# A decoder layer on one core: two side tiles moved from the delta solve to the convolution, and the first of them split by VectorE

## What is computed

```
proj = xn @ w_in                                   # one combined input projection
qkv, gate_a, b, a, q_b, k_b, v_b, gate_b, sel_a, sel_b = split(proj)
qkv = silu(causal_conv(qkv, conv_w, width 4))      # 12 channel tiles of 128
q, k = l2norm(q), l2norm(k)
o_a = gated_delta(q, k, v, beta, logd)             # chunks; (L + I)^-1 per chunk and head
...                                                # retention on q_b, k_b, v_b; merge; experts
```

## Time and profile before

| | |
|---|---|
| median of 3 runs | 2220.53 us (2217.37 to 2221.3) |
| the profiled execution | 2223.61 us, its span 2221.8 us |
| TensorE busy | 1816.8 us (82%) |
| VectorE busy | 1311.0 us (59%) |
| ScalarE busy | 878.0 us (40%) |
| GpSimd busy | 635.9 us (29%) |
| convolution | from 159.6 to 258.05 us |
| delta solve | from 258.05 to 438.3 us |

### The profile page before, as it was taken

The page is one execution under the profiler, slowest core; times in us unless marked ns, Lnnn a source line. Parts: engine busy times, 40 slices in busy tenths (PEclk is TensorE's granted clock), DMA queues, the critical chain, the costliest instruction groups (busy, mean ns, idle before and its releaser), DMA issues.

```text
span 2221.8 us, 25857 instructions
## 1 busy us (share of the span) xinstructions
PE 1816.8 (82%) x8652; PEld 1172.6 (53%) x8652; DVE 1311.0 (59%) x2832; ACT 878.0 (40%) x2277; POOL 635.9 (29%) x553
## 2 busy tenths in 40 slices
PE   5988889979987897899887777777777777777776
PEld 4988889969967887565542222222223222222222
DVE  2228363353364527677866766767667866766764
ACT  4223312242244224444444444444444444444443
POOL 0003012100000002454434344444444443444442
PEclk8999899979997997999999999999999999999999
DMA  3413112236015229999999999999999999999997
GB/s 102 126 42 92 34 51 72 76 106 201 26 67 191 94 75 369 332 405 410 419 393 420 417 419 420 420 419 416 404 420 400 419 419 419 406 420 420 420 410 294
DMA packets 171790, 636.84 MB, mean 287 GB/s; under 512 B 12531, under 2 KB 97590, under 8 KB 104713
## 3 DMA queue, kind: packets, MB, share of 16 engines
q0 software_dynamic: 74880, 545.29, 60.0%
q1 hardware_dynamic: 96784, 89.98, 13.0%
HBM read 617.39 MB, written 17.93 MB: 286 GB/s over the span
## 4 chain that ended last, share of the span: by engine, by line
DMA 31%; PE 12%; ACT 8%; DVE 8%; issue 3%; POOL 0%; DVEq 0%; POOLq 0%; ACTq 0%
DMA ex_uv_row<-in_peer_uv,ex_eidx 31%; PE ps L2037 9%; DVE ex_uv_row L2270 5%; ACT ex_spread L2129 2%; ACT L2119 2%; ACT L2113 1%; ACT ret_tables L2124 1%; PE ps L612 1%; PE ps L614 1%; PE ps L613 1%; ACT ret_tables L2119 1%; DMA ex_uv_row<-in_peer_uv,ex_eidx_s 1%; DVE ex_sel L2242 0%; DVE ex_sel L2246 0%; DVE ex_best L2245 0%
## 5 line engine op out<-in xcount | busy, mean ns | idle before, releaser
L2037 PE MATMUL ps<-ex_uv_row,ex_spread 128*128 128x512 f32 (+1 forms) x2020 | 964.7, 611 | 278.9 <-ACT ex_spread L2129 276.6
L1996 POOL DMA_INDIRECT ex_uv_row<-in_peer_uv,ex_eidx x512 | 564.3, 1102 | 999.7 <-PE ps L2037 711.4
L2270 DVE CUSTOM_DVE_ANT_0 ex_uv_row<-ex_uv_row,x_ffn 128x1024 f32<-128x1024 f32 x512 | 623.9, 1224 | 361.4 <-DMA ex_uv_row<-in_peer_uv,ex_eidx 355.6
L2037 PEld LDWEIGHTS ps<-ex_uv_row,ex_spread 128*128 128x128 f32 (+1 forms) x2020 | 351.5, 189 | 852.7 <-issue 852.4
L2119 ACT ACTIVATE ret_tables<-ret_tables 128x1 f32<-128x1 f32 x520 | 104.9, 202 | 645.7 <-DVE ret_tables L2270 644.2
L2129 ACT ACTIVATE ex_spread<-square,ret_tables 128x128 f32<-128x128 f32 (+1 forms) x505 | 201.9, 400 | 16.6
L2124 ACT ACTIVATE ret_tables<-ret_tables 128x1 f32<-128x1 f32 x512 | 150.6, 294 | 17.0
L612 PE MATMUL ps<-proj_b_whi,x_lo 128*128 128x256 f32 (+1 forms) x320 | 91.0, 285 | 7.6 <-DVE proj_b_wlo L521 7.0
L612 PE MATMUL ps<-x_hi,ex_w_lo 128*128 128x260 f32 (+1 forms) x272 | 90.7, 333 | 6.3 <-DVE x_lo L2313 3.3
L614 PE MATMUL ps<-proj_b_whi,x_hi 128*128 128x256 f32 (+1 forms) x320 | 90.6, 283 | 0.0
L613 PE MATMUL ps<-proj_b_wlo,x_hi 128*128 128x256 f32 (+1 forms) x320 | 90.5, 283 | 0.0
(11 more groups left out here) (409 smaller groups left out, 3245.3 us busy)
## 6 DMA issues: line engine op xcount, KB each, us to landing
first_raw<-in_w_in SPq DMA_DIRECT2D x8, 1024.0 KB, 8.3
ex_uv_row<-in_peer_uv,ex_eidx POOLq DMA_INDIRECT x512
dp_w_raw<-in_w_in SPq DMA_DIRECT2D x14, 512.0 KB, 4.3
proj_a_raw<-in_w_in SPq DMA_DIRECT2D x4, 1024.0 KB, 5.2
cv_w_raw<-in_w_in SPq DMA_DIRECT2D x8, 512.0 KB
proj_b_raw<-in_w_in SPq DMA_DIRECT2D x4, 1024.0 KB, 5.7
S_sample<-in_state_ret SPq DMA_DIRECT2D x1, 4096.0 KB, 22.4
out_ret_s<-S_sample SPq DMA_DIRECT2D x4, 1024.0 KB, 4.4
```

Of the source, the lines that this page charges most:

```text
L1996: pool.indirect_dma_start(uv_row[:, p % RING, :], None, a["peer_uv"][0], bass.IndirectOffsetOnAxis(ap=index_of(n), axis=0)).then_inc(row_l ...
L2037: ins = pe.matmul(k.pv[j % 2][0:r, c, :], spread[:, p % RING, 0:r], uv_row[:, p % RING, D + c * 512:D + (c + 1) * 512], start=first, stop= ...
L2270: dve.tensor_tensor_reduce(u, u, x, 1.0, 0.0, ALU.mult, ALU.add, coef[:, n:n + 1]).then_inc(dotted, 1)
```

## The change

Two side tiles go from `delta_solve` to `convolve`: 10 there and 12 in the solve. In `convolve` the first tile's split is done by VectorE, as the first instruction of its program, where GpSimd did it; GpSimd begins with tile 1, and waits for the first split so that the counts stay in order. The other two phases with side tiles keep their form.

```diff
-SIDE_BESIDE = {"ba": 2, "cv": 8, "dp": 14}
+SIDE_BESIDE = {"ba": 2, "cv": 10, "dp": 12}
...
-    def on_gpsimd(self, pool):
-
-        for n in range(len(self.tiles)):
+    def split_first(self, dve):
+
+        dve.wait_ge(self.rounded, 1)
+        dve.tensor_tensor(self.w_lo[0][:, :, :], self.raw[0][:, :, :],
+                          self.w_hi[0][:, :, :].bitcast(F32), ALU.subtract).then_inc(self.split, 1)
+
+    def on_gpsimd(self, pool, first=0):
+
+        for n in range(first, len(self.tiles)):
             pool.wait_ge(self.rounded, n + 1)
+            wait(pool, self.split, first)
             pool.tensor_tensor(self.w_lo[n % 2][:, :, :], self.raw[n % 2][:, :, :],
                                self.w_hi[n % 2][:, :, :].bitcast(F32), ALU.subtract).then_inc(self.split, 1)
...
             @block.gpsimd
             def _(pool):
-                side.on_gpsimd(pool)
+                side.on_gpsimd(pool, 1)
...
             @block.vector
             def _(dve):
                 own = Own(dve, dve_own)
+                side.split_first(dve)
                 dve.wait_ge(st_turned, 1)
```

## The result

The changed kernel takes 2230.99 us (median of 4 runs, 2227.34 to 2231.69), the kernel before 2220.91 us (4 runs). The ratio is 1.0039, its 95% interval 1.0022 to 1.0056: slower by 8.7 us by the ratio (4.9 to 12.4), by the two medians 10.1. The forecast was 2227.2 us, slower by 6.7. The profiled execution of the changed kernel took 2227.34 us, its span is 2225.3, so it is the fastest of the four.

A forecast was written before the change was run, and what follows sets the result against it. Phases end at barriers; VectorE paces the convolution's channels, TensorE's chain with side halves the solve's last level. Split +2.4, convolution tiles +12.9, solve -8.6 give +6.7 us on 2220.53: 2227.2 us, range 2220.5 to 2233.

The forecast's parts named there:

- The last level: Solve's last level: its four steps lose their half, each going from 4.66 to 2.73 us, saving 7.7 us.
- Rival (c): Solve's last level drops to 1.2 GHz without the halves, saving only the store's 0.9; 2234.9 us, chance 0.12.
- The late store's part: Barrier behind the solve: the last side store is issued some 10 us before the end, saving 0.9 us.
- The four halves: Convolution: four added halves come after VectorE's last channel, 11.6 us, with delays 12.9; bounds 11.6 to 14.6.
- rival (d): Convolution: the two tiles vanish beside VectorE, only 2.4 us is lost, kernel gains 6.2; 2214.3 us, chance 0.06.
- tile 9's landing: Convolution: tile 9's load, issued at about 221.1, lands 4.3 us later and delays half 17 by 0.4.
- VectorE's split: Convolution's head: the split delays state taps, tails and SP's third load, making channels 2.4 us late; bounds 0.1 to 4.1.
- The step that named SP's load as what decides: Convolution: tile 2's load waits for the tails, so its rounding is 2.4 us late and holds VectorE's channel 2.
- Rival (a): Convolution: late tails cost nothing as tensor_tensor passes the split, +0.1 instead of +2.4; 2224.9 us, chance 0.12.
- Rival (b): Sums behind the squares: denser halves keep the clock up, total +1.7 us; 2222.2 us, chance 0.12.
- the term of 8.6: Delta solve: two tiles fewer save 7.7 us in the last level and 0.9 from the earlier last store.

The follow-up runs named there:

- the kernel with early loads: Changed kernel with every load from the fourth on issued once its buffer is split, ahead of the store it used to follow; 2227.57 us, one run.
- mixing: Late split, ten tiles, with the last four halves placed between the eight sums of squares on TensorE; 2230.54 us, ratio 1.0055 to the kernel before.
- the kernel with quarters in level 0: Kernel before, with a quarter of side product in all four level 0 steps instead of two, copies one half ahead; 2223.69 us, ratio 1.0012.
- the early loads, on top of the mixing: Late split, ten tiles, last four halves between the sums of squares, plus loads issued once their buffer is split; 2217.32 us, one run.
- with eight tiles the same: Late split, eight tiles, early loads, last two halves mixed with the first four sums of squares; 2223.64 us, ratio 1.0009 to the kernel before.

## Why the prediction was right, and where it was off

*The last level.* A step took 2.74 us at clock 1.00 for 2.73. That it is right to the hundredth is in part luck: ScalarE's copy was handed on after 0.05 us for the 0.15 of the estimate, and the next L1081 followed after 0.99 for 0.88. Rival (c), that it loses its clock, fell with this window. The late store's part was 0.8 for 0.9. The solve as a whole took 7.1 to 9.9 us less than the 180.3 of before in the seven profiles with twelve tiles (mean 8.4) for 8.6; the differences lie ahead of the last level, and go with the time at 1.2 GHz.

*The four halves.* The step was right in mechanism: they stand bare between the last SiLU and the squares, and rival (d) fell. Its term was somewhat small: 13.7 and 14.2 us for 12.9 (18.3 and 18.9 less 4.6). The part that was off is tile 9's landing, 5.4 and 5.9 us for 4.3; the kernel with early loads shows it. It lay within the bounds of 11.6 to 14.6.

*VectorE's split.* The last SiLU is at 57.6 to 58.8 in the four profiles with GpSimd's split (mean 58.3) and at 59.7 to 60.5 in the five with VectorE's at the head (mean 60.1): +1.8 for the +2.4 of the sum. tensor_tensor was held, as chosen between the bounds, but for 2.0 and not 2.35 us, and in the changed kernel the first tile was rounded 5.1 and 5.3 us behind its load where the profile that the sum started from had 5.8. The step that named SP's load as what decides is only half true: without it VectorE's own delay gives nearly the same. Rival (a) fell: the tails were not free. The rule of the Trainium skill ("SBUF — State Buffer", section "Who interferes with whom"), that a VectorE instruction with two SBUF inputs blocks against a GpSimd instruction reading SBUF, holds here for tensor_tensor too (2.29 for 0.28 us). The prediction spoke of instructions with two SBUF operands, but others were held in the same way: a tensor_scalar (1.93 us for 0.48 at 179.29) and, in the solve of before, a copy of 128x4 (2.28 for 0.16).

*The clock.* Rival (b) fell: the clock fell behind the squares in both profiles of the changed kernel, as before the change. What I left out is that the length of the slow stretches differs from execution to execution, and the phases with it. From the first square to the solve it takes 34.7 to 35.1 us in the six profiles without mixing that have 13.7 us at 1.2 GHz there, and 36.1 to 36.5 in the five with 17 us. For the solve (the kernel with quarters in level 0 left out):

| at 1.2 GHz in the solve, us | solve with 14 tiles, us | solve with 12 tiles, us |
|---|---|---|
| 7.4 | 178.1 | |
| 10.2 to 10.7 | 178.9 | 170.4, 170.8, 171.2 |
| 13.7 | 180.3, 180.3, 180.3 | 171.7 |
| 16.9 to 17.4 | 181.6 | 173.0, 173.1, 173.2 |

At equal slow time two tiles less are worth 8.1 to 8.6 us of the solve, which bears out the term of 8.6 better than the two profiles with 9.9 and 7.1 do by themselves.

With the means of the two profiles of each kernel the sum is +1.8 (to the last SiLU) +14.0 (to the squares) +1.1 (to the solve) -8.5 (solve) = +8.3 (from times that are not rounded), for the measured +8.7. Against my +6.7 that is 1.1 more in the four halves, 0.6 less in the split, 1.1 in the sums behind the squares and 0.1 in the solve. The difference lies within the interval. The longer stretches come with either number of tiles, so nothing here says that the changed kernel draws them more often; with so few profiles it stays open. The first profile of before, on which the sum was made, was itself 2.4 us slower than the median of 29 runs (2223.61 against 2221.22); I carried its terms over to the median.

*A slip in rival (d).* For the kernel to be told from no change as faster, more than 11.1 of the 12.9 us would have to be hidden (-6.2 + 1.8 = -4.4), not 8.5. The four halves cost 13.7 and 14.2, so nothing hangs on it.

## What to carry to other kernels

Filler work costs its full length as soon as it stands behind the work that hid it: count how many pieces the cover ties to itself (here one half per SiLU) before adding any, and compare with what the last user of the filler really saves without it (1.9 us a step for a half of 2.9). An instruction put at the head of an engine's program delays all that used to run in the shadow of the load it waits for. And before a stretch of thin matmuls, look whether a late load leaves TensorE idle: here the early loads, on top of the mixing, took 9 us off the phase in one profile, though with eight tiles the same did not help, so this is a thing to try and not a rule. Before reading a difference of a few us from two profiles, compare the time at 1.2 GHz in the stretch: here it moved a phase by up to 2.8 us with nothing changed.

## What the runs showed of the hardware

- TensorE can be entered as busy and yet lose its clock: in a window that one-column matmuls mostly fill it was busy for 13.50 of 13.50 us at a granted clock of 0.50. The clock fell behind the squares in every profile but that of ten tiles mixed with early loads, for 13.7 to 17.1 us in all. What in this stretch brings it down is not settled.
- A dependent chain with gaps kept it: busy 8.25 of 11.00 us at 1.00, in the last level of the solve.
- The same kernel's runs spread over 14 us (2215.4 to 2229.2 for the kernel before). In the profiles the part of this that falls in the two phases goes with the time at 1.2 GHz behind the squares and in the solve; for the rest of the kernel that is not shown.
- VectorE's instructions that met a whole GpSimd split took 2.0 to 2.1 us longer, also those with one data operand: a tensor_tensor 2.29 for 0.28, a tensor_scalar 2.59 for 0.48 (at 169.96 before), a copy 2.28 for 0.16.
- A phase that ends with a store pending starts the next one 3.06 or 3.07 us behind the issue of that store (260 KB), in seven profiles; with no store pending it is 1.1 behind the last instruction.
- Tile 9's load of 512 KB was used 5.4 to 6.2 us after its issue in five profiles, where the median landing in the solve was 4.3. That it stands directly behind a store does not explain it: from the fourth on the solve's loads do so too, and in the changed kernel's convolution two other loads directly behind such a store were used on landing 4.0 us (issue 179.70) and 5.8 us (issue 185.45) after their issue. The cause stays open.
